# Decayed operands of three head pairs prepared among the last dense units, substitution steps placed among attention

## The reference, cut to what matters

```python
def hybrid_layer(x, ...):
    p = rmsnorm(x, norm_g) @ w_in                 # r, k, v, lora, gates, q_down, kv_down, k_idx
    y_rwkv = rwkv7_branch(...); y_attn = dsa_branch(...)
    return x + concatenate([y_rwkv, y_attn]) @ w_out

# rwkv7_branch: token shift of r, k, v; 8 heads of 64
decay = exp(-exp(-softplus(-(w0 + tanh(wd) @ w_up)) - 0.5))
a = sigmoid(a0 + ad @ a_up)
kk = k * k_k;  kk = kk / maximum(sqrt(sum(kk * kk)), 1e-12)
k = k * (1 + (a - 1) * k_a)
for each token:                                    # state S, 64 x 64 per head
    S = S * w_t + (S @ -kk_t) (kk_t * a_t)^T + v_t k_t^T;  y_t = S @ r_t
y = groupnorm(y) + sum(r * k * r_k) * v            # the bonus
# dsa_branch: index scores, top 128 keys per query, softmax attention of 8 heads over them
```

## Time and profile before

| | us |
|---|---|
| median of 3 runs | 1495.29 (1492.29 to 1496.96) |
| the profiled execution | 1498.92 |
| its span (first to last instruction) | 1497.2 |
| PE busy | 1427.7 (95%) |
| DVE busy | 959.8 (64%) |
| ACT busy | 493.0 (33%) |
| POOL busy | 487.7 (33%) |

### The profile page before, as it was taken

One profiled execution on the slowest core, in us unless ns is written; L12 is line 12 of the kernel. 1 busy time (PEld: TensorE's weight loads), 2 busy tenths in 40 slices (PEclk: granted clock), 3 DMA queues, 4 the chain that ended last, 5 costly groups with the idle time before them and its releaser, 6 DMA issues.

```text
span 1497.2 us, 18597 instructions
## 1 busy us (share of the span) xinstructions
PE 1427.7 (95%) x7596; PEld 1159.2 (77%) x7596; DVE 959.8 (64%) x1329; ACT 493.0 (33%) x669; POOL 487.7 (33%) x132
## 2 busy tenths in 40 slices
PE   8999988689999999999999999989989999999997
PEld 6778656577888787788888887768878888888886
DVE  6679867633654466659978974673357888885121
ACT  5443376243343333222222223322134333332121
POOL 0004110002544332334344443325333344443441
PEclk9999999678998999999999999999989999999998
DMA  6221000103323221122323222222321322222221
GB/s 202 85 85 57 29 2 2 65 22 113 113 85 113 85 84 57 60 109 85 112 86 106 91 88 81 84 84 84 111 87 56 113 84 100 98 89 102 90 87 56
DMA packets 21348, 125.12 MB, mean 84 GB/s; under 512 B 2384, under 2 KB 3408, under 8 KB 7696
## 3 DMA queue, kind: packets, MB, share of 16 engines
q1 hardware_dynamic: 20752, 121.71, 22.8%
q10 hardware_dynamic: 512, 2.23, 0.4%
HBM read 121.84 MB, written 2.10 MB: 83 GB/s over the span
## 4 chain that ended last, share of the span: by engine, by line
PE 88%; DVE 7%; ACT 3%; issue 1%; DMA 0%; POOLq 0%; POOL 0%; DVEq 0%; SPq 0%; ACTq 0%
PE bank L400 25%; PE bank L401 24%; PE bank L402 24%; PE bank L982 1%; PE bank L998 1%; PE bank L352 1%; PE bank L382 1%; DVE op_lo L1722 1%; ACT w_hi L1231 1%; ACT prob L1384 1%; DVE conv_b L2360 1%; PE bank L669 1%; PE bank L391 1%; PE bank L875 0%; PE bank L682 0%
## 5 line engine op out<-in xcount | busy, mean ns | idle before, releaser
L1178 POOL TENSOR_TENSOR w_lo<-w_raw,w_hi 128x2048 fp32r<-128x2048 f32 (+1 forms) x102 | 467.1, 4579 | 791.2 <-ACT w_hi L1231 774.0
L400 PE MATMUL bank<-op_hi,w_hi 128*128 128x512 f32 x1344 | 531.6, 396 | 13.5 <-DVE op_lo L1701 6.7
L401 PE MATMUL bank<-op_lo,w_hi 128*128 128x512 f32 x1344 | 527.3, 392 | 0.0
L402 PE MATMUL bank<-op_hi,w_lo 128*128 128x512 f32 x1344 | 527.1, 392 | 0.0
L400 PEld LDWEIGHTS bank<-op_hi,w_hi 128*128 128x128 f32 x1344 | 254.5, 189 | 72.1 <-issue 11.2
L1231 ACT ACTIVATE w_hi<-w_raw 128x2048 fp32r<-128x2048 f32 (+2 forms) x109 | 205.7, 1887 | 282.2 <-PE bank L402 282.1
L402 PEld LDWEIGHTS bank<-op_hi,w_lo 128*128 128x128 f32 x1344 | 254.2, 189 | 54.8
L401 PEld LDWEIGHTS bank<-op_lo,w_hi 128*128 128x128 f32 x1344 | 254.5, 189 | 54.1 <-issue 0.7
L2252 DVE SCALAR_TENSOR_TENSOR bank<-pad_b,par,bank 128x512 f32<-128x512 f32 x232 | 175.3, 756 | 7.8
L2419 DVE TENSOR_TENSOR tmp<-tmp,conv_f 128x512 f32<-128x512 f32 x22 | 101.5, 4615 | 16.4 <-ACT tmp L1647 16.4
L2160 DVE TENSOR_TENSOR x_res<-bank,x_res 128x512 f32<-128x512 f32 x24 | 16.5, 691 | 108.8 <-PE bank L402 108.7
(11 more groups left out here) (365 smaller groups left out, 1739.3 us busy)
## 6 DMA issues: line engine op xcount, KB each, us to landing
w_raw<-in_w_units SPq DMA_DIRECT2D x104, 1024.0 KB, 4.8
w_raw<-in_w_units SPq DMA_DIRECT2D x4, 768.0 KB, 4.1
x_res<-in_x SPq DMA_DIRECT2D x8, 256.0 KB, 6.4
x_res<-in_x ACTq DMA_DIRECT2D x2, 1024.0 KB, 6.2
out<-x_res SPq DMA_DIRECT2D x8, 256.0 KB, 2.3
w_raw<-in_w_units SPq DMA_DIRECT2D x3, 512.0 KB, 9.2
w_raw<-in_w_units SPq DMA_DIRECT2D x4, 256.0 KB, 5.6
mem_tok<-in_mem SPq DMA_DIRECT2D x1, 1024.0 KB, 4.8
```

The costliest lines, as they stand in the source:

```text
L400: nc.tensor.matmul(b[:, 0:width], h, xh[:, x0 + k, 0:width], start=start and k == ks[0], stop=False)
L401: nc.tensor.matmul(b[:, 0:width], h, xl(x0 + k, width), start=False, stop=False)
L402: mm = nc.tensor.matmul(b[:, 0:width], l, xh[:, x0 + k, 0:width], start=False, stop=stop and k == ks[-1])
L1178: nc.gpsimd.tensor_tensor(w_lo[u % 2][:, 0:nk, :], w_raw[u % 2][:, 0:nk, :], w_hi[u % 2][:, 0:nk, :].bitcast(F32), ALU.subtract).then_inc( ...
```

## The change

- The sums for the key lengths are made in two halves (pairs 0 and 1, pairs 2 and 3), each between the tiles of a dense unit: r1 and g1. So are the root and the reciprocal.
- The inputs of pairs 0, 1 and 2 (`pair_inputs`) and their bonuses go between tiles of k1, v1, g1, ga0, ga1 on PE; `decay_and_rate`, `decays`, `key_terms` and `decayed` follow in ACT's and DVE's lists; POOL's `decayed` stand between its `split_lo`. Top-k rounds are distributed anew, more of them ahead of r1.
- Pair 3 is prepared first in the attention stage. All four `strict_upper` come before the first `heads_out`.
- The 31 steps of the substitution are spread among attention (0 to 6, 10, 14, 20, 31), `value_grams(1)` on DVE comes after `blocks_out`, and `chunk_values(1)` on PE and ACT after the side products.

```diff
-unit_tiles("r", 1, oh, ol)
-for what in "kvg":
-    unit_tiles(what, 1, oh, ol)
...
+def key_sums(half):
+    b = bank(("kk", half))
+    pe.wait_ge(sem("consts"), 5)
+    pe.wait_ge(sem("kk_sq"), 2 * half + 2)
+    for j in range(2):
+        for c in range(NT):
...
+    done(mm, ("kk", half))
...
-    pe.wait_ge(sem("kk_tok_ready"), 1)
+    pe.wait_ge(sem("kk_tok_ready"), i // 2 + 1)
...
-unit_tiles("ga", 0, oh, ol)
+def pair_inputs(i):
+    decay_and_rate(i)
+    norms_spread(i)
+
+unit_tiles("r", 1, oh, ol, between=lambda: key_sums(0))
 pe.wait_ge(sem("lora_loaded"), 16)
-decay_and_rate(0)
-norms_spread(0)
-unit_tiles("ga", 1, oh, ol)
-key_bonus(0)
-
+unit_tiles("k", 1, oh, ol, between=lambda: pair_inputs(0))
+unit_tiles("v", 1, oh, ol, between=lambda: key_bonus(0))
+pair_inputs(1)
+unit_tiles("g", 1, oh, ol, between=lambda: key_sums(1))
+key_bonus(1)
+unit_tiles("ga", 0, oh, ol, between=lambda: pair_inputs(2))
+unit_tiles("ga", 1, oh, ol, between=lambda: key_bonus(2))
...
+pair_inputs(3)
 head_inputs(0)
-decay_and_rate(1)
...
+strict_upper(0)
 scores(0)
-strict_upper(0)
+strict_upper(1)
+key_bonus(3)
+head_inputs(1)
+strict_upper(2)
+scores(1)
 head_values()
-key_bonus(1)
-for p in range(1, NI):
-    head_inputs(p)
-    scores(p)
-    if p + 1 < NI:
-        decay_and_rate(p + 1)
-        norms_spread(p + 1)
-    strict_upper(p)
-    if p + 1 < NI:
-        probabilities_turned(p - 1)
-        heads_out(p - 1)
-        key_bonus(p + 1)
+strict_upper(3)
+probabilities_turned(0)
+heads_out(0)
+head_inputs(2)
+scores(2)
+probabilities_turned(1)
+heads_out(1)
+head_inputs(3)
+scores(3)
...
 heads_out(NI - 2)
 chunk_values(0)
 probabilities_turned(NI - 1)
+heads_out(NI - 1)
 token_major(1)
 value_grams(1)
-heads_out(NI - 1)
-chunk_values(1)
 pe.wait_ge(sem("blocks_out"), 2)
 side_products(0)
 side_products(1)
+chunk_values(1)
 token_major(2)
...
-for u in range(FIRST_POOL_UNIT, first_phase2_unit):
-    split_lo(u)
...
+split_lo(FIRST_POOL_UNIT)
+split_lo(FIRST_POOL_UNIT + 1)
+decayed(0)
+split_lo(FIRST_POOL_UNIT + 2)
+decayed(1)
+split_lo(FIRST_POOL_UNIT + 3)
+decayed(2)
+filled(pool, ("ga", 1, 1))
+step(nc.gpsimd.memset(m_blk[:, :, :], 0.0))
+diagonal = m_blk[:, :, :].rearrange("p s t -> p (s t)")[:, 0:BLK * BLK:BLK + 1]
+nc.gpsimd.memset(diagonal, 1.0).then_inc(sem("m_started"), 1)
+decayed(3)
...
+            elif (half, w, m) == (1, 0, 0):
+                key_norms(0)
+            elif (half, w, m) == (1, 1, 0):
+                act.wait_ge(sem("relu_used"), 12)
+                decay_and_rate(0)
+                decays(0)
...
+    if half:
+        decay_and_rate(1)
+        decays(1)
...
+key_norms(1)
 for half in range(2):
     for m in range(2):
         b = take(act, ("ga", half, m))
         evacuated(act, ("ga", 0, m) if half else ("g", 1, m))
         A(sig_t[m][:, :], b[:, :], ACT.Sigmoid).then_inc(sem("sig_g"), 1)
+        if (half, m) == (0, 0):
+            decay_and_rate(2)
+            decays(2)
     u += 1
     split_hi(min(u + 1, first_phase2_unit - 1))
-    if half == 0:
-        act.wait_ge(sem("relu_used"), 12)
-        decay_and_rate(0)
-        decays(0)
...
+decay_and_rate(3)
 head_inputs(0)
-decay_and_rate(1)
+decays(3)
 strict_upper(0)
-decays(1)
+strict_upper(1)
+exps(0)
+head_inputs(1)
+strict_upper(2)
 head_values()
-exps(0)
-for p in range(1, NI):
-    head_inputs(p)
-    if p + 1 < NI:
-        decay_and_rate(p + 1)
-    strict_upper(p)
-    if p + 1 < NI:
-        turned(p - 1)
-        decays(p + 1)
-        exps(p)
+strict_upper(3)
+turned(0)
+exps(1)
+head_inputs(2)
+turned(1)
+exps(2)
+head_inputs(3)
...
-chunk_values(1)
 for half in range(2):
     evac(A(z5[quarter(1), half, :], take(act, ("zA", half))[quarter(1), :], ACT.Copy), ("zA", half))
+chunk_values(1)
...
-        else:
-            topk_rounds((22, 30, 37)[w])
...
-    topk_rounds((13, 43)[half])
...
+def key_norms(half):
+    k = kk_tok[:, 4 * NT * half:4 * NT * half + 4 * NT]
+    evacuated(dve, ("kk", half))
+    link(V.tensor_scalar(k, k, 2e-12, None, ALU.max))
+    V.reciprocal(k, k).then_inc(sem("kk_tok_ready"), 1)
...
+            elif (half, w, m) == (1, 0, 1):
+                key_norms(0)
+            elif (half, w, m) == (1, 1, 0):
+                shifted(0)
+                key_terms(0)
+            elif (half, w, m) == (1, 2, 0):
+                decayed(0)
...
+        split_lo(u + 1)
...
+        elif (half, w) == (0, 1):
+            index_scores(2)
+            topk_rounds(6)
+        elif (half, w) == (0, 2):
+            index_scores(3)
+            topk_rounds(14)
+        else:
+            topk_rounds((32, 34, 38)[w])
+    if half:
+        key_terms(1)
...
+    if half:
+        key_norms(1)
+    topk_rounds((24, 41)[half])
+for half in range(2):
+    if half == 0:
+        decayed(1)
     for m in range(2):
...
+        if (half, m) == (0, 0):
+            shifted(1)
+            key_terms(2)
+        elif (half, m) == (1, 0):
+            decayed(2)
     u += 1
     split_lo(min(u + 1, first_phase2_unit - 1))
-    if half == 0:
...
-        key_terms(0)
+    topk_rounds((46, 48)[half])
...
-decayed(0)
...
-key_terms(1)
+key_terms(3)
 maxima(0)
-decayed(1)
-for p in range(1, NI - 1):
-    if p >= 2:
-        heads_out(p - 2)
-    maxima(p)
-    probs(p - 1)
-    key_terms(p + 1)
-    decayed(p + 1)
-heads_out(NI - 3)
-maxima(NI - 1)
-probs(NI - 2)
+decayed(3)
+maxima(1)
+probs(0)
 blocks_in()
-substitution(0, 8)
-probs(NI - 1)
+substitution(0, 6)
+heads_out(0)
+maxima(2)
+probs(1)
+substitution(6, 10)
+heads_out(1)
+maxima(3)
+probs(2)
+substitution(10, 14)
 value_grams(0, 0)
 value_grams(0, 1)
 heads_out(NI - 2)
-substitution(8, 16)
+probs(3)
+substitution(14, 20)
+heads_out(NI - 1)
+substitution(20, BLK - 1)
+blocks_out()
 value_grams(1, 0)
 value_grams(1, 1)
-heads_out(NI - 1)
-substitution(16, BLK - 1)
-blocks_out()
```

More of the change, by code:

```diff
@@ L541, in _ @@
             unit_tiles("g", 0, oh, ol)
-            unit_tiles("r", 1, oh, ol)
-            for what in "kvg":
-                unit_tiles(what, 1, oh, ol)
[L545 to L552, removed]
+            def key_sums(half):
[4 more added lines that the diff above has]
+                    for c in range(NT):
+                        n = 2 * NT * j + 2 * c
+                        mm = nc.tensor.matmul(b[:, n:n + 2], kk_sq[:, 2 * half + j, c * P:c * P + P], pair_ones[:, 0:P:HD],
+                                              start=True, stop=True)
+                done(mm, ("kk", half))
             def decay_and_rate(i):
@@ L1179, in split_lo, with decayed @@
                                         w_hi[u % 2][:, 0:nk, :].bitcast(F32), ALU.subtract).then_inc(lo_ready, 1)
-            for u in range(FIRST_POOL_UNIT, first_phase2_unit):
-                split_lo(u)
-            for i in range(NI):
+            def decayed(i):
                 e_up = tmp[1][:, 0:516].rearrange("p (c t) -> p c t", c=NT)[:, :, 1:P + 1]
@@ L1316, in relus, with decay_and_rate, decays @@
                     evac(A(prep[n % 4][:, 0:w], take(act, ("lg", qt, h))[:, 0:w], ACT.Relu), ("lg", qt, h))
+            def decay_and_rate(i):
+                if i:
+                    act.wait_ge(sem("prep_ready"), i)
+                    act.wait_ge(sem("bk_decayed"), 2 * i)
+                evac(A(prep[0][:, 0:T], take(act, ("z", i))[:, :], ACT.Tanh, scale=0.5, bias=half_wa[:, i:i + 1]), ("z", i))
+                evac(A(prep[1][:, 0:T], take(act, ("a", i))[:, :], ACT.Tanh, scale=0.5, bias=half_wa[:, NI + i:NI + i + 1]), ("a", i))
+                evacuated(act, ("a", i))
+                A(rs[:, :], prep[1][:, 0:T], ACT.Identity, scale=half_ka[:, i:i + 1], bias=omka[:, i:i + 1]).then_inc(sem("rate_ready"), 1)
+            def decays(i):
+                act.wait_ge(sem("cum_ready"), i + 1)
+                A(tmp[0][:, 0:516], prep[2][:, 0:516], ACT.Exp, scale=-0.5 * KAPPA).then_inc(sem("exps"), 1)
+                A(tmp[1][:, 0:516], prep[2][:, 0:516], ACT.Exp, scale=0.5 * KAPPA).then_inc(sem("exps"), 1)
+            def key_norms(half):
+                n = 4 * NT
+                evac(A(kk_tok[:, n * half:n * half + n], take(act, ("kk", half))[:, 0:n], ACT.Sqrt, scale=4.0), ("kk", half))
             u = 3
@@ L1943, in decayed, with key_norms @@
                 V.tensor_tensor(chunked(ar[:, i, 1, :]), chunked(ar[:, i, 1, :]), e_down[:, :, 1:P + 1], ALU.mult).then_inc(sem("prep_ready"), 1)
-            evacuated(dve, "kk")
-            link(V.tensor_scalar(kk_tok[:, :], kk_tok[:, :], 2e-12, None, ALU.max))
-            V.reciprocal(kk_tok[:, :], kk_tok[:, :]).then_inc(sem("kk_tok_ready"), 1)
-            for half in range(2):
+            def key_norms(half):
+                k = kk_tok[:, 4 * NT * half:4 * NT * half + 4 * NT]
+                evacuated(dve, ("kk", half))
+                link(V.tensor_scalar(k, k, 2e-12, None, ALU.max))
+                V.reciprocal(k, k).then_inc(sem("kk_tok_ready"), 1)
@@ new lines, in shifted @@
+            def shifted(half):
```

(42 more changed lines are left out.)

45 lines of the change are left out of this document (removed).

## The result

The changed kernel takes 1502.2 us (median of 10 runs, 1496.5 to 1506.4) where the kernel before took 1495.5 in the same session (10 runs, 1492.3 to 1497.9): a ratio of 1.0043, 95% interval 1.0028 to 1.0057. The forecast was 1494.5 us, with 1485 to 1502. The time is 0.2 us outside the range, and the change goes the other way than I forecast.

What follows compares the result with a forecast made beforehand. PE was taken as the bound (88% of the last chain). 2.2 us gained at the side products less 1.4 for clock behind new waits made 0.8 us faster: 1494.5 us in terms of the median, range 1485 to 1502.

Steps and rivals of the forecast that it cites:

- Gain 2.2 us: Side products and `chunk_values(1)` behind them done at 280.3 instead of 282.5, with the key lengths' 3.0 us of clock included.
- the 0.8 gained: Whole kernel: the forecast's sum, 2.2 us gained less 1.4 us for clock, so 0.8 us faster.
- The level behind the 9.4 us wait is as now.: PE behind the wait at L720, ahead of the side products: granted clock claimed unchanged, about half.
- the key lengths in halves: Units r1 and g1 on PE: splitting the tiny matmuls removes the half-clock stretch behind them, 3.0 us gained.
- The bounds of ±3.0: Key lengths on PE: 3.0 us gained if neither half drops the clock, 3.0 lost if both do.
- the waits: PE: 1.7 us at the first norms, 3.5 at the first bonus, 5.4 at the scores, 9.4 at the side products.
- the third dense wait: PE in the dense units: norms of pair 2 are out 1.2 us late.
- POOL's queue: DVE beside POOL's 4.6 us splits: `decayed(0)` given 5.6 us, `key_norms(1)` waits 2.6 for ACT's root and 3.1 for POOL.
- the clock behind the new waits: PE behind the 3.5 us wait and the 5.4 us scores wait: 0 to 5 us lost to lower clock, 1.4 taken.
- DVE is in time: Rival, 31%: POOL's splits hold DVE little, `scores(0)` ends 6 us earlier and everything after it too: 1488.5 us.
- The split of unit 10 is late: Rival, 23%: ACT's `decays(0)` waits for DVE's `cum`, delaying unit 10's high part, so g1 waits too: 1502 us.

Runs made afterwards that it cites:

- experiment 6, before_busy: The kernel before with 13 useless matmuls added on PE in the 12.6 us wait ahead of the side products: 1491.4 us, ratio 0.9975.
- experiment 7, after_busy: The changed kernel with 10 useless matmuls added on PE in the 9.4 us wait ahead of the side products: 1490.9 us, ratio 0.9972.
- experiment 5, values_late: The kernel before with only the change's tail: `chunk_values(1)` behind the side products, `value_grams(1)` on VectorE behind `blocks_out`: 1500.9 us, ratio 1.0040.
- experiment 4, values_first: The changed kernel with `chunk_values(1)` put back ahead of the side products: 1495.6 us, ratio 1.0006.
- experiment 2, halves: The kernel before with only the key lengths in two halves, between tiles of r1 and g1: 1498.6 us, ratio 1.0023.
- experiment 8, halves_busy: The kernel before with the key lengths in halves and 13 useless matmuls ahead of the side products: 1496.0 us, ratio 1.0003.
- after: The changed kernel itself, in its first measurement and profile: 1502.2 us, ratio 1.0043, profiled span 1497.5 us.
- after_again: The changed kernel run again without any edit, for a second profile: 1503.2 us, ratio 1.0065.
- terms_first: values_first with VectorE's `key_terms(3)` ahead of the last two top-k rounds instead of behind them: 1491.2 us, ratio 0.9973.
- terms_busy: terms_fill with 5 useless matmuls added on PE ahead of the side products: 1487.6 us, ratio 0.9953.
- terms_busy2: terms_busy with 3 more useless matmuls ahead of the first bonus in the dense stage: 1488.1 us, ratio 0.9948.
- before: The kernel before the change, without edits: 1495.5 us in the first session, profiled span 1497.2 us.
- terms_fill: terms_first with four more substitution steps ahead of `heads_out(3)` on VectorE: 1490.5 us, ratio 0.9968.
- rounds_later: The changed kernel with fewer early top-k rounds, 22 for 24 behind g0 and 29 for 32 in half 1: 1505.6 us, ratio 1.0072.

## Why the prediction was wrong, step by step

*Failed: "Side products start at 273.2 ... and `chunk_values(1)`, now behind them, to 280.3. Before, the same work was done at 282.5. Gain 2.2 us."* This is the step that failed. Side products did start at 272.3. `chunk_values(1)` was given 3.5 us (276.8 to 280.3), about the 3.7 of its rows ahead of the wait, while the side products right before it were taken at the 3.6 us that they have at half clock. Behind a 9.4 us wait both run at half clock, and `chunk_values(1)` measures 6.8 us. Moved from ahead of a wait to behind it, the same matmuls went from free to nearly double price. The sign follows from this step: the 3.3 us turn the 0.8 gained into 2.5 lost. With the clock held, the kernels are level (experiments 6 and 7), the tail alone costs 5.9 us (experiment 5), and taking it back gives 7.6 (experiment 4). The other 4.2 of the 6.7 us aren't in this sum; see below.

*Failed with it: "The level behind the 9.4 us wait is as now."* The level is (0.53), but the work that it lies on grew by 3.7 us.

*Right in mechanism, without worth: the key lengths in halves, "+3.0".* The low stretch went, but PE, earlier by 2.7 us, then waited 2.9 for VectorE's norms. Alone, the halves cost about 4 us (experiments 2 and 8). The bounds of ±3.0 were about the clock only; what is late next wasn't asked. What the halves are worth inside the full change, where VectorE's list is another, no run shows by itself.

*Right: the waits.* 3.2 and 5.4 us in the places named, 9.4 for 12.6 at the side products, and 1.2 at the first norms; the third dense wait, 1.2 us, is only 0.2.

*Right in place, too large in part: POOL's queue.* VectorE's norms and first product of decay fall into POOL's splits (POOL's L1186 runs 136.12 to 140.74 and 158.94 to 163.52):

```profile
139.51 1.24 DVE L1934 TENSOR_TENSOR misc<-tmp,tmp 128x3 f32<-128x3 f32 x1
...
160.39 3.16 DVE L1945 TENSOR_SCALAR kk_tok<-kk_tok 128x16 f32<-128x16 f32 x1 [2.54 <-ACT kk_tok L1348]
```

The waits of 2.6 and 3.1 us were forecast for the second. It ends with the split; the same instruction takes 0.17 us where no split runs (experiment 2). `decayed(0)` takes 3.4 us (139.5 to 142.9), for the 5.6 that it was given. The Trainium skill (GPSIMD Engine Reference, Specifications) has contention with VectorE's instructions that have two SBUF inputs or run in a 2-port performance mode. The trace agrees for the first kind: 1.24 us for the 128x3 product, where the same line takes some 0.16 for the other pairs. The key norms have one tensor input and took 3.16 us; whether they run in such a mode the trace doesn't tell.

*Not one number: the clock behind the new waits ("I take 1.4").* Behind the 3.2 us wait single executions show 1.00 over 134:142 (after), 0.79 (after_again, values_first) or 0.57 (after_busy). From one half of the key lengths to the other this makes 44.7, 46.3 and 46.2, or 47.5 us: a cost of none, 1.6 or 2.8. Behind the scores all have 0.84 over 184:206, for 0.92 in the kernel before. So in most of these profiles 1.4 is too little. values_first, which has all of these waits, is 1.3 us above the kernel before all the same, with an interval that includes none.

*The rivals.* "DVE is in time" is refuted by the waits. "The split of unit 10 is late" had the time right (1502) and the reason wrong: g1 waits for no `w_lo`. No rival of mine spoke of work moved behind a wait; it could be read from the earlier trace rows, where 278.9:287.5 has 0.55 with PE always busy.

*Where more of it lies.* From the start of `side_blocks` to the end of the span, all fourteen profiles (the kernel before, the changed one and the twelve runs above) take one of few times. Seven take 1204.8 to 1205.8 us (halves, values_late, before_busy, halves_busy, terms_first, terms_busy, terms_busy2). Six take 1209.3 to 1210.0 (before, after, after_again, values_first, after_busy, terms_fill), and rounds_later takes 1211.3. Each has a stretch of half clock that begins 4 to 6 us behind that start: it lasts some 3.5 us in the seven, some 13.5 in the six and 17 in the last. The window 288:308 of terms_first, then of terms_fill:

```profile
288.00:308.00 20.00, 20.00 (x243) 17.52 (x240) 8.20 (x13) 8.42 (x16) 0.00 (x0) 0.91 0.42 159
...
288.00:308.00 20.00, 20.00 (x184) 17.28 (x184) 5.28 (x9) 7.03 (x13) 0.00 (x0) 0.66 0.42 159
```

terms_fill starts `side_blocks` 1.4 us before terms_first (282.3 for 283.6) and has a span 3.3 us longer. So an execution pays some 4.5 us more or not, in a place that none of the edits touches. That is as large as most differences measured here. With the cost of none to 2.8 us behind the first bonus it is large enough for the 4.2 us that the failed step leaves; that it is the cause of them isn't shown.

*Open.* What decides between the short and the long stretch, and how often each kernel has the long one: one profile for each kernel doesn't show it.

## What to carry to other kernels

Price a moved instruction at the clock of the place it goes to: ahead of a long wait of PE it may be free, behind it it can cost twice its time. Where a wait can't be removed, give it work that needs nothing from the wait, or matmuls that nobody reads, and see whether the stretch behind it runs faster. And before crediting the removal of a slow stretch, ask which engine's list lies beside it: if that list decides, the gain becomes a wait, and the wait may bring the slow clock back. Read, too, how long the slow stretches are in each profile before two kernels are compared by their spans.

## What was not expected of the hardware

- Useless work made both kernels faster: 26 passes (11.4 us) in a wait of 12.6 us gave 3.6 us, 8.9 us in a wait of 9.4 gave 11.3. The Trainium skill (TensorE: Matmul & The Clock Gate, HAM oscillation) says that a long wait for data leaves the next burst of matmuls cold, at the lower clock. The trace agrees, with 0.53 behind 9.4 us.
- In the changed kernel PE was busy without a break from 272.3 us on, with side products, small value products and transposes, and stayed at the lower level (1.2 GHz) to about 287. The forecast priced `chunk_values(1)` as if the higher one were back at once. In terms_busy the clock even fell during such work, behind a wait of only 0.8 us (0.57 over 276:280).
- The times of one kernel spread with the mean granted clock of the execution: the changed kernel from 1496.5 us at 0.969 to 1506.4 at 0.961, about 1.2 us for each 0.001. Two profiles of one kernel can differ by more than a change of this size is worth.
